# The first gate slab of six merges: split and multiplied inside the attention stage that comes before

## The reference, cut to what matters

```python
aq, ak, av, az, bq, bk, bv, bo, bz, bg, cq, ck, cv, cz, gm = split_proj(h @ w_in)
y_a = diff_head_norm(diff_attn_blocks(...)) * silu(az)     # "da"
y_b = mlstm_out(h_b, bo, bz, ml_g)                          # "mlstm"
y_c = neighbourhood_attn(...) * silu(cz)                    # "na"
proj = jnp.einsum('btnw,nwd->btnd', y, w_br)
g = jax.nn.sigmoid(gm.reshape(gm.shape[:2] + (N_BRANCH, -1)))
x = x + gate * (jnp.sum(g * proj, axis=2) @ w_out)
```

## Time and profile before

| | |
|---|---|
| median of 3 runs | 3180.71 us (3179.9 to 3181.45) |
| the profiled execution: its time | 3175.28 us |
| its span, first to last instruction | 3173.6 us, mean granted PE clock 0.982 |
| PE busy | 3014.3 us (95%) |
| PE weight loads busy | 2451.3 us (77%) |
| DVE busy / ACT busy / POOL busy | 1479.9 / 1156.0 / 146.1 us |

### The profile page before, as it was taken

How to read it: one execution, slowest core, us unless ns; L and a number is a source line. 1 busy time by engine, 2 the same in 40 slices (tenths; PEclk the granted TensorE clock), 3 DMA queues, 4 the chain that set the end, 5 groups by cost and what they waited for, 6 DMA issues and landing times.

```text
span 3173.6 us, 38627 instructions
## 1 busy us (share of the span) xinstructions
PE 3014.3 (95%) x15614; PEld 2451.3 (77%) x15614; DVE 1479.9 (47%) x1970; ACT 1156.0 (36%) x1822; POOL 146.1 (5%) x206
## 2 busy tenths in 40 slices
PE   7999999999999999998999799989999899989988
PEld 5777888777788877867888688858877688878666
DVE  4645455544454556374342622253445644432444
ACT  4334233534343343154232521262222634331442
POOL 1000000100000000000000400100000000300100
PEclk9999999999999999999999999999999999999999
DMA  4243332330322221101111311312111022221312
GB/s 174 93 149 116 106 119 83 127 133 27 134 92 104 95 80 60 54 21 43 46 61 67 87 66 40 109 29 73 53 60 60 24 68 86 93 86 64 106 67 80
DMA packets 44454, 256.71 MB, mean 81 GB/s; under 512 B 6344, under 2 KB 6352, under 8 KB 20512
## 3 DMA queue, kind: packets, MB, share of 16 engines
q1 hardware_dynamic: 30528, 204.30, 18.3%
q0 software_dynamic: 13792, 50.51, 4.9%
HBM read 250.51 MB, written 4.28 MB: 80 GB/s over the span
## 4 chain that ended last, share of the span: by engine, by line
PE 85%; DVE 7%; ACT 3%; DMA 2%; issue 1%; POOL 1%; SPq 0%; DVEq 0%; ACTq 0%; POOLq 0%
PE PS L732 14%; PE PS L733 14%; PE PS L734 14%; PE PS L713 7%; PE PS L712 7%; PE PS L714 7%; PE PS L678 2%; PE PS L676 2%; PE PS L677 2%; DVE SMALL L2306 1%; PE PS L913 1%; DMA W<-in_w 1%; PE PS L1007 1%; PE PS L1023 1%; PE PS L997 1%
## 5 line engine op out<-in xcount | busy, mean ns | idle before, releaser
L732 PE MATMUL PS<-HHX,WHX 128*128 128x512 f32 (+1 forms) x1600 | 567.9, 355 | 40.8 <-DVE WLM L2156 31.3
L733 PE MATMUL PS<-HL,WHX 128*128 128x512 f32 (+1 forms) x1600 | 568.4, 355 | 0.0
L1480 ACT ACTIVATE WHX<-W 128x2048 fp32r<-128x2048 f32 x108 | 186.1, 1723 | 613.4 <-DMA W<-in_w 391.4
L732 PEld LDWEIGHTS PS<-HHX,WHX 128*128 128x128 f32 x1600 | 309.3, 193 | 86.2 <-issue 33.2
L734 PE MATMUL PS<-HHX,WLX 128*128 128x512 f32 (+1 forms) x1024 | 357.2, 349 | 0.0
L733 PEld LDWEIGHTS PS<-HL,WHX 128*128 128x128 f32 x1600 | 307.5, 192 | 41.4
L2156 DVE TENSOR_TENSOR WLX<-W,WHX 128x2048 fp32r<-128x2048 f32 x60 | 137.5, 2292 | 382.3 <-ACT WHX L1480 382.3
L713 PE MATMUL PS<-HL,WH 128*128 128x512 f32 x672 | 265.4, 395 | 0.0
L712 PE MATMUL PS<-HH,WH 128*128 128x512 f32 x672 | 263.3, 392 | 0.0
L714 PE MATMUL PS<-HH,WL 128*128 128x512 f32 x672 | 261.7, 389 | 0.0
L2156 DVE TENSOR_TENSOR WL<-W,WH 128x2048 fp32r<-128x2048 f32 x68 | 155.9, 2292 | 221.7 <-ACT WH L1480 221.7
(11 more groups left out here) (494 smaller groups left out, 5688.1 us busy)
## 6 DMA issues: line engine op xcount, KB each, us to landing
W<-in_w SPq DMA_DIRECT2D x172, 1024.0 KB, 4.7
XC<-in_wm POOLq DMA_DIRECT2D x12, 1024.0 KB, 5.1
H<-in_wm POOLq DMA_DIRECT2D x12, 1024.0 KB, 5.7
W<-in_wb SPq DMA_DIRECT2D x24, 512.0 KB, 3.2
W<-in_w SPq DMA_DIRECT2D x8, 768.0 KB, 4.2
ARENA<-mrow POOLq DMA_DIRECT2D x12, 256.0 KB, 4.0
ARENA<-wrow POOLq DMA_DIRECT2D x12, 256.0 KB, 4.3
PR<-in_nbias POOLq DMA_DIRECT2D x12, 256.0 KB, 3.0
```

What stands on the lines that cost most here:

```text
L732: pe.matmul(dst, wh[:, s, c], hi[:, k, t0:t1], start=k == 0, stop=False)
L733: pe.matmul(dst, wh[:, s, c], lo[:, k, t0:t1], start=False, stop=False)
L1480: act.activation(dst[:, s, 0:n], W[:, s, 0:n], ACT.Copy).then_inc(wh_ready[s], 1)
```

## The change

Each attention stage now knows the merge behind it (`st.merge`). Four things change.

1. **Splits.** Slab 0 of the merge's unit 0 is split during the attention, in two halves of 128x1024 each (`act_head`, `dve_head`), into memory that is free there (`head_slab`: MF, MFV, XCR, SELR, parts of ACCL, WHX, WLM, WLX). In da both ACT halves stand ahead of all exponentials and both DVE halves behind the first two maxima. In mlstm the ACT halves stand at the end of passes 9 and 10 in layer 0 (it has passes 0 to 7 over the latent tokens, then the shorter 8 to 15 over the context) and of passes 2 and 3 in layer 1 (0 to 7 alone), the DVE halves one pass later. In na they stand 10 and 8 steps (ACT), 6 and 4 steps (DVE) ahead of the end.
2. **The product.** `pe_head` makes slot 0 of unit 0 in parts: part 0 and part 1 are 24 matmuls of 128x512 each, part 2 (layer 0 alone) 48 of 128x256. They stand between the last products and turns of the attention.
3. **The merge** on ACT and DVE no longer splits slab 0 at its start, and PE's loop runs over units 1 to 3, with slot 1 of unit 0 ahead of it.
4. **Banks and memory.** In mlstm the PSUM banks 0/1 and 6/7 change places, so that the product can have 0 and 1; PE waits for all eight banks before its first scores, where it waited for six. Some scratch moves.

```diff
+    def act_head(act, st, part):
+        act.wait_ge(w_ready[0], 16 * (st["it"] + 1))
+        ins = act.activation(head_slab(st)[part][0], raw_half(part), ACT.Copy)
+        if part == 1:
+            ins.then_inc(wh_ready[0], 1)
...
+    def dve_head(dve, st, part):
+        dve.wait_ge(wh_ready[0], st["ws"] + 1)
+        hi, lo = head_slab(st)[part]
+        ins = dve.tensor_tensor(lo, raw_half(part), hi.bitcast(F32), ALU.subtract)
+        if part == 1:
+            ins.then_inc(wl_ready[0], 1)
...
+    def pe_head(pe, st, part):
+        if part == 0:
+            pe.wait_ge(wl_ready[0], st["ws"] + 1)
...
+        for m in range(m0, m1):
+            dst, cols = (PS[:, m, :], slice(0, T)) if lat else (PS[:, 4, m * TC:(m + 1) * TC], slice(T, TA))
+            for k in range(KT):
+                hi, lo = (v[:, k % 4, m * P:(m + 1) * P] for v in halves[k // 4])
+                pe.matmul(dst, hi, HHX[:, k, cols], start=k == 0, stop=False)
+                pe.matmul(dst, hi, HL[:, k, cols], start=False, stop=False)
+                mm = pe.matmul(dst, lo, HHX[:, k, cols], start=False, stop=k == KT - 1)
...
             if n < nj:
                 transposes(jobs[n])
+            else:
+                pe_head(pe, st.merge, n - nj)
             if 0 <= n - 2 < nj and jobs[n - 2]["last"]:
                 turn(jobs[n - 2])
+        if st.merge.ctx:
+            pe_head(pe, st.merge, 2)
...
+            if e["s"] == len(steps) - 1:
+                pe_head(pe, st.merge, 0)
             transposes(e)
             if e["s"]:
                 values(steps[e["s"] - 1])
+        if st.merge.ctx:
+            pe_head(pe, st.merge, 1)
         values(steps[-1])
+        pe_head(pe, st.merge, 1 + st.merge.ctx)
...
-        for b in range(6):
+        for b in range(8):
             wait_free(pe, st, b, 0)
...
+        pe.wait_ge(sem("ml_c"), past("ml_c", ly) + 3 * n_lat)
+        pe_head(pe, st.merge, 0)
         pe.wait_ge(sem("ml_y"), past("ml_y", ly) + np_ // 2 - 1)
         turn(passes[-1])
+        for part in range(1, 2 + st.merge.ctx):
+            pe_head(pe, st.merge, part)
...
-        with pe.Fori(0, 4) as i:
+        pe_split_unit_x(pe, st, 0, YTH, YTL, (sem("y_lo"), 4 * merge_no(st) + 1), 4, (1,))
+        with pe.Fori(1, 4) as i:
...
-        if not st.after_norm:
+        if not st.after_norm and st.kind != "merge":
             act_split(act, st, 0, 0)
```

More of the change, by code:

```diff
@@ L72, in __init__ @@
         self.norm_next = None
+        self.merge = None
         self.after_norm = False
@@ L236, in plan_stages @@
     for i, st in enumerate(out):
+        if st.kind in ("da", "mlstm", "na"):
+            st.merge = out[i + 1]
         if st.kind == "fox":
@@ L436, in build @@
     cv = Carve(scratch)
-    DM1, DM2, DM3, QS1, QS2, QS3 = (cv(T) for _ in range(6))
+    QS1, QS2, QS3 = (cv(T) for _ in range(3))
     KTX = cv(8, P)
+    DM1, DM2, DM3 = (cv(T) for _ in range(3))
     assert cv.at <= hyb_at + 2 * KT * SLAB
@@ L527, in split_bufs, with head_slab @@
         return HHX, HL, WHX, WLX, TA
+    def head_slab(st):
+        if st.n == 0:
+            halves = [(MF[:, 0, :], MF[:, 1, :])] * 2
+        elif st.layer:
+            halves = [(ACCL[:, :, T:TA], XCR[:, :])] * 2
+        elif st.n == 1:
+            halves = [(WHX[:, 0, :], MFV[:, :])] * 2
+        else:
+            halves = [(WLX[:, 1, 4 * SLAB:8 * SLAB], WLM[:, 0, 0:4 * SLAB]),
+                      (SELR[:, :], WLM[:, 0, 4 * SLAB:8 * SLAB])]
+        whole = halves[0] == halves[1] or not (st.layer == 0 and st.n == 2)
+        out = []
+        for part in range(2):
+            pair = []
+            for v in halves[part]:
+                if len(v.shape) == 2:
+                    v = v.rearrange("p (a b) -> p a b", b=SLAB)
+                pair.append(v[:, 4 * part:4 * part + 4, :] if whole else v)
+            out.append(pair)
+        return out
@@ new lines, in raw_half @@
+    def raw_half(part):
+        return W[:, 0, 4 * SLAB * part:4 * SLAB * (part + 1)].rearrange("p (a b) -> p a b", b=SLAB)
+    def act_head(act, st, part):
[9 more added lines that the diff above has]
+            ins.then_inc(wl_ready[0], 1)
@@ new lines, in pe_head @@
+    def pe_head(pe, st, part):
+        if part == 0:
+            pe.wait_ge(wl_ready[0], st["ws"] + 1)
+        halves = head_slab(st)
+        lat = part < 2
+        m0, m1 = (part, part + 1) if lat else (0, 2)
+        for b in (0, 1, 2, 3) if part == 0 else ():
+            wait_free(pe, st, b, 0)
+        if not lat:
+            wait_free(pe, st, 4, 0)
+        for m in range(m0, m1):
[5 more added lines that the diff above has]
+                mm = pe.matmul(dst, lo, HHX[:, k, cols], start=False, stop=k == KT - 1)
+            if lat:
+                mm.then_inc(full[m] if m == 0 or st.ctx else slab_used[0], 1)
+            elif m == 1:
+                mm.then_inc(slab_used[0], 1)
@@ L1625, in act_da @@
         act.preload_act_table_set("natural_log_exp_and_others")
+        for part in range(2):
+            act_head(act, st.merge, part)
         exps(jobs[0])
@@ L1661, in act_na @@
                 exps(steps[e["s"] + 2])
+            if len(steps) - e["s"] in (10, 8):
+                act_head(act, st.merge, int(len(steps) - e["s"] == 8))
     def act_merge(act, own, st):
@@ L1777, in act_mlstm @@
                 divide_forward(it)
+            if p in (heads, heads + 1):
+                act_head(act, st.merge, p - heads)
         squares(passes[-1])
@@ L2351, in dve_da @@
         maxima(jobs[1])
+        for part in range(2):
+            dve_head(dve, st.merge, part)
         for n in range(nj + 3):
@@ L2403, in dve_na @@
                 post(steps[e["s"] - 2])
+            if len(steps) - e["s"] in (6, 4):
+                dve_head(dve, st.merge, int(len(steps) - e["s"] == 4))
         for e in steps[-2:]:
@@ L2614, in dve_mlstm @@
                 scale(passes[p - 1])
+            if p in (heads + 1, heads + 2):
+                dve_head(dve, st.merge, p - heads - 1)
         scale(passes[-1])
```

31 lines of the change are left out of this document (19 added, 12 removed).

## The result

The changed kernel takes 3136.3 us (median of 4 runs, 3133.6 to 3141.0) where the kernel before, run beside it, takes 3180.3 (3177.0 to 3181.5): a ratio of 0.9865 with the interval 0.9848 to 0.9882, 1.3% faster. The forecast was 3140.4. The profiled execution took 3136.75 us, where the sum in the prediction had 3135.0 for it; its span is 3135.0, and was 3173.6.

The account below looks back on a forecast made before the run. PE was taken to idle in each attention's tail, waiting for the slab's low part, and return at a lower clock. Gains 48.4 less costs 8.1 gave 40.3 us: 3180.7 to 3140.4, own range 3132 to 3152, 8 in 10 3129 to 3158.

Parts of the forecast that it names:

- da, layer 0: Tail of da in layer 0: 27.8 us become 18.4, gain 9.4; late first probabilities cost 2.2.
- na: Tails of na: gains 8.4 in layer 0 and 8.6 in layer 1; splits cost 0, hidden in slack.
- da, layer 1: Tail of da in layer 1: stretch 21.0 to 17.0, 2.2 for waking, gain 1.8; split cost 2.2.
- mlstm, layer 1: Tail of mlstm in layer 1: 24.5 us become 11.7, gain 12.8; halves cost 2.2, between 0 and 4.5.
- mlstm, layer 0: Tail of mlstm in layer 0: 27.0 us become 19.6, gain 7.4; halves cost 1.5, between 0 and 4.5.
- Here the clock was already at the lower level: Mlstm, layer 0, at part 0's place: low clock makes part 0 cost 5.5 + 2.1 = 7.6 us.
- The exchange of banks: Start of mlstm: PE waits 1.3 to 2 us longer at worst, but POOL sets the pace; 0, at most 2 per layer.
- Rival A: All attentions: splits not hidden, 4.5 us each and 2 more at mlstm's start, costs 31; time 3163. Chance 0.15.
- Rival C: All tails: product runs at the lower clock level, 72 us more than forecast, 3212. Chance 0.04.
- Rival D: Tails: slot 1 waits for a y chain lengthened as much as the slab came earlier; 3175 to 3181. Chance 0.03.
- B: All attentions: splits cost nothing because the pipelines recover, gain 48.4, time 3132. Chance 0.12.

Follow-up runs that it names:

- e2: Changed kernel with DVE's two slab halves ahead of the first maxima of da instead of behind the second: 3132.7 us, ratio 0.9858.
- e4: Changed kernel with mlstm's first pass reordered on PE, so that it waits only for the banks it needs: 3134.1 us, ratio 0.9859.
- e8: Changed kernel with each of DVE's two halves in mlstm carried out twice: 3145.6 us, ratio 0.9887.
- e3: Changed kernel with the last turn of da in layer 1 between the product's two portions instead of behind both: 3130.1 us, ratio 0.9851.
- e10: The changed kernel run once more, unedited ("again" in the table): 3136.1 us, ratio 0.9868.
- e6: Changed kernel with both da edits, DVE's halves ahead of the first maxima and layer 1's last turn between the portions: 3124.5 us, ratio 0.9826.
- e11: e9 with DVE's halves of mlstm in layer 0 one pass later: 3123.5 us, ratio 0.9829.
- e5: Kernel before with only mlstm's exchange of banks and the wait for all eight: 3181.1 against 3179.1 us, ratio 1.0002 over 12 runs.
- e9: e6 with e4's order at the start of mlstm: 3125.1 us, ratio 0.9830.
- e1: Changed kernel with the early split kept, but all product portions issued after the attention's last turn or values: 3149.3 us, ratio 0.9907.
- e7: e6 with ACT's and DVE's halves in mlstm of layer 1 two passes earlier: 3125.1 us, ratio 0.9832.

## Why the prediction was right, and where it was not

The mechanism is the one forecast, and the time came within 4.1 us: a gain of 40.3 was forecast, 38.6 is it between the spans of the two profiled executions, 44.0 between the medians. Of that difference little is the prediction's doing: the profiled execution of before was 5 us faster than the other runs of that kernel beside it, and the medians of before lay between 3176.4 and 3180.3 from one set of runs to the next.

That the net is so near is in part luck. Measured as the prediction counts, from part 0's place to the product of y, the six stretches of after are 50.6 us shorter than before (2.0 of waking behind da in layer 1 taken off), where it had 48.4; and part 0 comes 12.7 us later in its attentions, where it had 8.1 for all costs. The two errors, 2.2 and 4.6 us, pull against each other. The costs in mlstm were the terms that were sized too small: 1.5 and 2.2, measured 3.4 and 4.2 in after.

By its own steps, with the table's gains (before less after, and before less again):

- **da, layer 0:** 9.4 less 2.2 is 7.2; measured 8.2. The late start was costed at 2.2, was 1.9 at the first transposes, and cost 1.5 at part 0 (e2); the pipeline regained the rest.
- **na:** 8.4 and 8.6; measured 7.7 to 7.8 and 8.3. Part 0 came 0.7 us and 0.1 us later than its place before: the splits cost next to nothing, as PE's full load said.
- **da, layer 1:** a stretch shorter by 4.0 less 2.2, and 2.2 of waking behind it. Measured 0.9 and 1.5, and 2.5 in e4 and e8, where the clock didn't fall early in the stage; 2.0 behind it (e3). The one idle gap of over 4 us was where the prediction put it, and with its length, 5.27.
- **mlstm, layer 1:** 12.8 less 2.2 is 10.6; measured 8.2 and 10.4. Part 0 came 2.0 us late in e3 and 2.4 in e10, near the 2.2 of the halves, but 4.2 in after. The trace of after shows what the rest is. Just ahead of part 0 PE waits 1.87 us; up to there after is 0.5 us behind e10. Behind that wait the clock falls to 0.50, and 1.4 more are lost, while in e10 it stays at 1.00 at the same place. In e6 (54.2) it falls there as well; in e2, e3 and e10 (50.7 to 51.1), with the same wait, it doesn't.
- **mlstm, layer 0:** 7.4 less 1.5 is 5.9; measured 6.5 and 5.9. The sum fits, and two terms in it were off against each other. "Here the clock was already at the lower level" was true of the kernel before and did not hold in after: part 0 ran at 1.00. That is 2 us more gain, and luck: the clock had fallen behind PE's wait of 2.44 us and rose 3.8 us ahead of part 0. In e8 and e11 part 0 did run at the lower level. Against it, part 0 came 3.4 us later in the stage than the same place before (58.1 against 54.8). 1.8 of that stands in e3 as well, and the rows under e11 show the half in it; the other 1.6 goes with the clock at the stage's start, by which the outputs start 1.5 later in after than in e3.
- **The exchange of banks** was taken at 0, at most 2 per layer. The wait it brings is 2.4, not 1.3 to 2, and the profile of after seemed to show it on the path in both layers. e5 and e9 say no within what the times can tell; that POOL's pace is what hides it fits the rows of e3 and e9 (POOL's next row after 9.7 and 9.4 us). What it can cost, 1.6 to 2.2 us in layer 0, goes with the clock that PE comes back with.

The two falls of the clock in after, ahead of part 0 in layer 0 and in layer 1:

```profile
1797.70:1801.00 3.30, 3.03 (x10) 2.44 (x11) 3.23 (x8) 1.89 (x10) 0.29 (x1) 0.50 0.26 40
2760.20:2763.50 3.30, 3.30 (x17) 3.28 (x16) 1.05 (x6) 0.79 (x4) 0.00 (x0) 0.50 0.00 0
```

Rival A (31 us of costs, 3163) falls with the time itself, and with e2, e5 and the na columns. Rival C (the product at the lower level) falls with the windows at 1.00, though e1 shows its smaller form, 1.2 to 2.0 us a tail. Rival D is what happened in one tail of six. The time lies midway between the forecast and B's 3132, but not for B's reason: e2 and the late part 0 of mlstm show that the splits cost.

Left open: why the clock falls behind the same wait in some executions and not in others, and what delays DVE beside POOL beyond one of its multiplies.

The kernel to keep is e6: two moves of a few lines in da, 3124.5 us, 1.7% under the kernel before. The times don't tell it from e7, e9 and e11 (3123.5 to 3125.1), which change more.

## What to carry to other kernels

When an operand of the next stage doesn't depend on this one, prepare it early: that alone was some 30 of 43 us here; weaving the product itself into the tail gave the rest, partly as waits filled and partly as clock kept. Put the independent work behind the last step that starts a dependent chain, not ahead of it, and give it at least the chain's length: one turn on the wrong side of a 5.7 us portion cost 7.4 us by the profile. A wait that a profile newly shows is no cost until it is removed by itself; here 2.4 us more of it in each layer cost the kernel before at most 3.2 us in all (e5), and 2.4 us less gained nothing that the times show (e9 against e6).

## What the runs showed of the hardware

After a wait of 3.27 us at the same place of the same program, PE's next eight matmuls took 2.04 us in some executions and 1.13 in others: nine kernels here have that wait in both layers, and ten of the 18 times it was 2.04 or 2.05, eight times 1.13 or 1.14. In four of these eight the clock fell right behind them, and the next eight matmuls took 1.47 to 1.90 us instead of 1.06:

```profile
2726.02 1.90 PE L1239 MATMUL PS<-ARENA 128*128 128x129 f32 x8
```

In the three kernels on the changed one that wait 0.88 us, and in the kernel before, they took 1.13 to 1.16 each time. Behind 5.03 to 5.31 us, in the kernel before and after, PE came back at the lower level each time, seven in all. And behind a wait of 1.87 us in mlstm of layer 1 the clock fell in after and e6 and stayed up in e2, e3 and e10, a difference of 1.4 us and more. A wait of such a middling length is thus a source of scatter as much as of delay. The same subtraction of 128x1024 took DVE 1.22 us alone, 1.86 (after) and 2.17 (e8) beside POOL's multiplies, and 3.82 (e7) over a multiply and the two DMA issues behind it; it ended 1.1 us behind these, about its own length.
